# Feed-forward down blocks: the left 512 columns as seven products of 2x2 block sums

## Chip, cores and metric
One core of a Trainium2 chip. The metric is the device time of one execution in microseconds (us); lower is better. The kernel before takes 1081.49 us, median of three runs (1081.03 to 1081.93).

## The reference
Two transformer-like layers on 256 tokens of width 1024, in fp32. The first begins with a feed-forward part (`x = x + 0.5 * rmsnorm(swiglu(rmsnorm(x)))`) and ends with another; between them lie gated attention and state-space branches and a cross attention to `mem`. The second layer (long convolutions from computed filters, and a latent attention) follows. What the change touches is

```python
def _swiglu(h, w_gu, w_down):
    g, u = jnp.split(h @ w_gu, 2, axis=-1)
    return (jax.nn.silu(g) * u) @ w_down
```

with a hidden width of 2816, so 22 hidden tiles of 128, and an output of 256 x 1024.

## The kernel before
All large products keep fp32 accuracy by halves. A value is rounded to TensorE's short fp32 form (the high half), the rest (the low half) is what is left of it, and a product is three: high by high, high by low, low by high (`product`, L527 to L529).

**Weights** come as a stream of blocks of 128 x 2048 fp32 (1 MB). SyncE fetches block b into `w_raw[b % 3]` once the low half of block b - 3 is made, ScalarE makes `w_hi` (`round_block`, L1378 to L1385) once the data are there and TensorE is done with block b - 3, and VectorE makes `w_lo` (`low_block`, L2105 to L2109). TensorE waits for `w_lo_in`. So every engine's queue is written out by hand, and each runs in its own order; semaphores alone tie them.

**A feed-forward part** (`ffn_part` on each engine; n = 1 and 2) has 22 up blocks (each gives one hidden tile: 48 products of 256 columns into one of eight banks of 512 fp32 columns) and 11 down blocks, each of two hidden tiles by 1024 output columns. Its order on TensorE is up 0, 1, 2, down 0, up 3, then eight turns of a loop of up 4, down 1, up 5 (names of the first turn), then up 20, down 9, up 21, down 10. A down block is, for each of its two hidden tiles k, four groups i (two halves of the tokens by two of 512 columns) of three products of 512 columns, into banks 3 to 6, in which they are summed over all blocks. For its last group some products are cut into 256 + 256 columns (L762, by the table `LAST_DOWN`). Up blocks rotate through banks 0 to 2, by block number.

**A hidden tile** (`hidden_tile`, L2237 on VectorE; `gate` and `high` on ScalarE) goes: VectorE multiplies the first half of the bank by the row scale `rb` (L2246), ScalarE takes silu (L1439), VectorE multiplies it with the second half (L2249, it frees the bank), ScalarE rounds it (L1448, for a tile from the third on after the down block that used the buffer), VectorE takes the low half (L2256). `hidden_tile` has two lists of weight blocks: those whose low halves are made between L2249 and L2256, and those behind it. The root of the rows' squares is turned by TensorE within up 2 (first part) or up 1 (second).

**Other work in these queues.** In the first part VectorE also scales `mem` (L2293, `mem_normal`) around tile 20, and its low halves (L2300) follow the last tile. In the second it folds the long-convolution filters around tiles 0 to 3 and 20 to 21 (`fold_decay` L2202, `fold_difference` L2207, `fold_sum` L2221). Behind the last down block come the squares (ScalarE, L1516), the gains (VectorE, L2342), the root and the residual (L2356). In the first part TensorE has the memory's key blocks `kv0` to `kv3` beside this, in the second `filter_spectrum` (L1049), whose results ScalarE copies, and then the transposes of the new x (L626, `raw_turn`).

At the start TensorE runs one fp32 product of zeros (`stay_warm`, L631), zeroes bank 0 (L702) and takes the first block in plain fp32 (L710).

## Time and profile before

| | |
|---|---|
| median of three runs | 1081.49 us |
| profiled execution | 1082.24 us |
| its span | 1080.5 us |
| TensorE busy | 1071.7 us (99%), 8574 products |
| VectorE busy | 786.1 us (73%) |
| ScalarE busy | 608.4 us (56%) |
| DMA | 190.71 MB, 177 GB/s in the mean |

The profile is one execution as the hardware profiler recorded it. PE is TensorE, PEld its weight loads, DVE VectorE, ACT ScalarE. L527 is line 527 of the kernel. Matmuls are pipelined, so the distance from one start to the next, not a row's own duration, tells what one costs. Idle time in brackets is that of the engine just before a row, with what ended it.

### The profile page before, as it was taken

The numbers are of one execution on the slowest core, as the hardware profiler recorded it, in microseconds if no ns is written. First come the engines' busy times: TensorE is split into PE (matmuls) and PEld (weight loads), VectorE is DVE, ScalarE is ACT, GpSimd is POOL, SyncE is SP. The second block draws the span as 40 slices with busy tenths as digits, with TensorE's granted clock in tenths as the row PEclk, the third lists the DMA queues.
The fourth block names the chain that finished last, engine by engine and source line by source line (L and its number), as shares of the span: only waits on it lengthen the run. The fifth ranks groups of instructions, "written<-read, shape, count | busy, mean of one in ns | idle before, by whom it ended". The sixth has DMA issues, their size and how long they took to land.

```text
span 1080.5 us, 21149 instructions
## 1 busy us (share of the span) xinstructions
PE 1071.7 (99%) x8574; PEld 1015.7 (94%) x8574; DVE 786.1 (73%) x1109; ACT 608.4 (56%) x905; POOL 0.2 (0%) x4
## 2 busy tenths in 40 slices
PE   8999999999999999999999999999999999999998
PEld 7999999999989999999999998999999799999998
DVE  5665657989979777778678556765555887997784
ACT  5544444678676545878446546444444576655561
POOL 0000000000000000000000000000000000000000
PEclk9999999999999999999999999999999999999999
DMA  9766556455443454454646533465555356543341
GB/s 347 287 220 207 181 180 211 155 207 181 172 156 119 157 176 157 157 178 138 214 160 242 196 116 128 138 234 194 194 192 197 118 177 211 179 157 118 118 156 39
DMA packets 29297, 190.71 MB, mean 177 GB/s; under 512 B 3656, under 2 KB 4521, under 8 KB 7466
## 3 DMA queue, kind: packets, MB, share of 16 engines
q1 hardware_dynamic: 26480, 182.53, 48.6%
q10 hardware_dynamic: 2746, 7.16, 1.9%
q8 instruction: 54, 0.88, 0.3%
q14 instruction: 17, 0.14, 0.0%
HBM read 188.62 MB, written 1.05 MB: 176 GB/s over the span
## 4 chain that ended last, share of the span: by engine, by line
PE 93%; DVE 3%; ACT 2%; DMA 1%; issue 1%; SPq 0%; DVEq 0%; ACTq 0%
PE bank L527 16%; PE bank L529 16%; PE bank L528 16%; PE bank L539 11%; PE bank L540 11%; PE bank L541 11%; PE bank L626 3%; PE bank L762 1%; DVE sb_w_lo L2109 1%; DVE sb_ssd_conv L2420 1%; DMA sb_w_raw<-in_w 1%; PE bank L710 1%; PE bank L887 1%; ACT sb_w_hi L1385 1%; PE bank L1257 1%
## 5 line engine op out<-in xcount | busy, mean ns | idle before, releaser
L2109 DVE TENSOR_TENSOR sb_w_lo<-sb_w_raw,sb_w_hi 128x2048 fp32r<-128x2048 f32 x169 | 386.5, 2289 | 128.9 <-ACT sb_w_hi L1385 128.2
L1385 ACT ACTIVATE sb_w_hi<-sb_w_raw 128x2048 fp32r<-128x2048 f32 x169 | 322.9, 1910 | 31.5 <-PE bank L529 28.2
L527 PE MATMUL bank<-sb_hT_hi,sb_w_hi 128*128 128x256 f32 (+1 forms) x816 | 226.2, 277 | 0.0
L529 PE MATMUL bank<-sb_hT_hi,sb_w_lo 128*128 128x256 f32 (+1 forms) x816 | 226.1, 277 | 0.0
L528 PE MATMUL bank<-sb_hT_lo,sb_w_hi 128*128 128x256 f32 (+1 forms) x816 | 226.0, 277 | 0.0
L539 PE MATMUL bank<-sb_hT_hi,sb_w_hi 128*128 128x256 f32 (+2 forms) x744 | 213.4, 287 | 0.2 <-DVE sb_hT_lo L2186 0.2
L540 PE MATMUL bank<-sb_hT_lo,sb_w_hi 128*128 128x256 f32 (+2 forms) x744 | 206.7, 278 | 0.0
L541 PE MATMUL bank<-sb_hT_hi,sb_w_lo 128*128 128x256 f32 x744 | 206.4, 277 | 0.0
L527 PEld LDWEIGHTS bank<-sb_hT_hi,sb_w_hi 128*128 128x128 f32 (+1 forms) x816 | 152.9, 187 | 0.0
L529 PEld LDWEIGHTS bank<-sb_hT_hi,sb_w_lo 128*128 128x128 f32 (+1 forms) x816 | 152.7, 187 | 0.1
L528 PEld LDWEIGHTS bank<-sb_hT_lo,sb_w_hi 128*128 128x128 f32 (+1 forms) x816 | 152.7, 187 | 0.0
L539 PEld LDWEIGHTS bank<-sb_hT_hi,sb_w_hi 128*128 128x128 f32 x744 | 140.2, 188 | 3.8 <-issue 2.4
L540 PEld LDWEIGHTS bank<-sb_hT_lo,sb_w_hi 128*128 128x128 f32 x744 | 140.0, 188 | 1.4 <-issue 1.2
L541 PEld LDWEIGHTS bank<-sb_hT_hi,sb_w_lo 128*128 128x128 f32 x744 | 139.9, 188 | 0.0
L1439 ACT ACTIVATE sb_ffn_gate<-sb_ffn_gate 128x256 f32<-128x256 f32 x44 | 18.4, 418 | 133.4 <-DVE sb_ffn_gate L2246 133.4
L527 PE MATMUL bank<-sb_w_hi,sb_ffn_hi 128*128 128x512 f32 x156 | 61.0, 391 | 0.4 <-DVE sb_ffn_lo L2256 0.4
L528 PE MATMUL bank<-sb_w_lo,sb_ffn_hi 128*128 128x512 f32 x156 | 60.9, 390 | 0.0
L529 PE MATMUL bank<-sb_w_hi,sb_ffn_lo 128*128 128x512 f32 x156 | 60.9, 390 | 0.0
L1448 ACT ACTIVATE sb_ffn_hi<-sb_ffn_act 128x256 fp32r<-128x256 f32 x44 | 18.3, 416 | 47.7 <-PE bank L762 34.7
L528 PE MATMUL bank<-sb_w_lo,sb_hT_hi 128*128 128x256 f32 (+1 forms) x136 | 40.0, 294 | 0.0
L529 PE MATMUL bank<-sb_w_hi,sb_hT_lo 128*128 128x256 f32 (+1 forms) x136 | 39.9, 294 | 0.0
L527 PE MATMUL bank<-sb_w_hi,sb_hT_hi 128*128 128x256 f32 (+1 forms) x136 | 39.9, 294 | 0.0
(518 smaller groups left out, 2087.0 us busy)
## 6 DMA issues: line engine op xcount, KB each, us to landing
sb_w_raw<-in_w SPq DMA_DIRECT2D x169, 1024.0 KB, 4.9
sb_w_raw<-in_w SPq DMA_DIRECT2D x4, 512.0 KB, 7.6
sb_hT<-in_xT SPq DMA_DIRECT2D x2, 512.0 KB, 5.3
sb_x<-in_x SPq DMA_DIRECT2D x2, 512.0 KB, 11.6
sb_mem_xn<-in_mem ACTq DMA_DIRECT2D x1, 1024.0 KB, 6.0
sb_mem_T<-in_memT ACTq DMA_DIRECT2D x1, 1024.0 KB, 8.3
sb_post_g<-in_ffn_post_g ACTq DMA_DIRECT2D x2, 512.0 KB, 5.2
sb_decay<-in_c_decay ACTq DMA_DIRECT2D x1, 768.0 KB, 4.3
```

Of the source, the lines that this page charges most:

```text
L527: pe.matmul(o, a_hi, b_hi, start=first, stop=False)
L528: pe.matmul(o, a_hi, b_lo, start=False, stop=False)
L529: return pe.matmul(o, a_lo, b_hi, start=False, stop=last)
L539: pe.matmul(o[:, 0:width + more[0]], stat_hi, moving(move_hi, width + more[0]), start=k == 0, stop=False)
L540: pe.matmul(o[:, 0:width + more[1]], stat_hi, moving(move_lo, width + more[1]), start=False, stop=False)
L541: return pe.matmul(o[:, 0:width], stat_lo, moving(move_hi, width), start=False, stop=k == kt - 1)
L626: return pe.transpose(o, src, ident)
L710: mm = pe.matmul(o[:, i * SEQ:(i + 1) * SEQ], w[:, k, i * P:(i + 1) * P], hT[:, k, :], start=False, stop=k == KD - 1 and i == 1)
L1385: act.activation(w_hi[b % STAGES][:], w_raw[b % RING][:], ACT.Copy).then_inc(w_hi_in, 1)
L1439: act.activation(f["gate"][:, j % 2, :], f["gate"][:, j % 2, :], ACT.Silu).then_inc(S("ffn_gate"), 1)
L1448: act.activation(f["hi"][:, j % 2, :], f["act"][:, j % 2, :], ACT.Copy).then_inc(S("ffn_hi"), 1)
L2109: tt(w_lo[b % STAGES][:], w_raw[b % RING][:], f32(w_hi[b % STAGES][:]), ALU.subtract).then_inc(w_lo_in, 1)
```

## The change
For the down blocks of the first ten tile pairs in each part, the left 512 output columns are computed by seven products of 2x2 block sums instead of eight products of blocks: token halves by hidden tiles by two groups of 256 columns. VectorE makes three sums of the block's weights as they land (`mix_block`), of 512, 256 and 256 columns, one of them in place of a block, and four sums of the hidden tiles (`first_sum`, `other_sums`), of 128 columns each. ScalarE and VectorE make the halves of these too (768 and 4 x 128 columns). Each of the seven products is, as before, three, of 256 columns; they are summed in four banks, 3 to 6, over the ten blocks. ScalarE copies three half banks and VectorE joins them once, ahead of the last hidden tile (`join`, seven operations of 256 columns). The right 512 columns stay products of 512, in bank 7 and a bank that up blocks used; up blocks keep two banks. The last down block is as before, into its own banks, and its left half is added to the joined one behind it. Three banks are zeroed by products of zeros, at the start of the kernel (fp32) or in the second part's first mixed block. The host orders the weights of these blocks anew. Changed lines, each group with its indentation taken off:

```diff
@@ -141,11 +141,13 @@
+MIXED_PAIRS = PAIRS - 1
+MIXED_OF = {down_at(n, c): MIXED_PAIRS * (n - 1) + c for n in (1, 2) for c in range(MIXED_PAIRS)}
@@ -329,7 +331,16 @@
+        "joined": place(40, f"ffn{n}_joined", [P, TOK, 512]),
+        "parts": place(44, f"ffn{n}_parts", [P, 3, 256]),
+mix_raw = place(40 + LINE, "mix_raw", [P, 768])
+mix_hi = place(43 + LINE, "mix_hi", [P, 768], F32R)
+mix_lo = place(46 + LINE, "mix_lo", [P, 768], F32R)
+sum_raw = place(49 + LINE, "sum_raw", [P, 4, P])
+sum_hi = place(51 + LINE, "sum_hi", [P, 4, P], F32R)
+sum_lo = place(53 + LINE, "sum_lo", [P, 4, P], F32R)
+zero_r = place(55 + LINE, "zero_r", [P, P], F32R)
@@ -655,7 +666,7 @@
-o = claim(f"rb{n}", 3)
+o = claim(f"rb{n}", 6)
@@ -664,7 +675,7 @@
-o = claim("mem_rb", 7)
+o = claim("mem_rb", (FIRST["ffn1"] + 1) % 3)
@@ -720,8 +731,17 @@
+def open_mixed(n, q):
+    claim(f"mixed{n}.{q}", 3 + q, down_at(n, MIXED_PAIRS - 1))
+    last_bank = (FIRST[f"ffn{n}"] + 2) % 3
+    def up_bank(j):
+        return last_bank if n == 1 and j == 2 else (FIRST[f"ffn{n}"] + j % 2) % 3
@@ -732,63 +752,129 @@
-            feature_block(f"up{n}.{j}", b, 2, hT_hi, hT_lo, ready=ready, between=between)
+            feature_block(f"up{n}.{j}", b, 2, hT_hi, hT_lo, bank=up_bank(j), ready=ready, between=between)
-        o = claim_turns([f"up{n}.{j + 2 * i}" for i in range(PAIR_TURNS)], b % 3, b, turn)
+        o = claim_turns([f"up{n}.{j + 2 * i}" for i in range(PAIR_TURNS)], up_bank(j), b, turn)
-    def down_block(c, turn=0, parts=(512,), all_three=False):
+    def mixed_block(c, turn=0, parts=(512,), all_three=False):
+        first, last = c == 0, c == MIXED_PAIRS - 1
+        hi, lo = w_hi[b % STAGES], w_lo[b % STAGES]
+        top, low = slice(0, P), slice(P, SEQ)
+        b11, u2, b22, b21 = (slice(i * 256, (i + 1) * 256) for i in range(4))
+        u1, u3, u4 = (slice(i * 256, (i + 1) * 256) for i in range(3))
+        def tile_in(k):
+            pe.wait_ge(S("ffn_lo"), FF_TILES * (n - 1) + 2 * c + 1 + k + 2 * turn)
+        def plain_half(o, k, t):
+            h = slice(1024 + k * 512, 1536 + k * 512)
+            return product(o[:], f["hi"][:, k, t], f["lo"][:, k, t], hi[:, h], lo[:, h], first and k == 0, False)
+        def of_tile(q, half, k, t, m_hi, m_lo, m, closes):
+            return product(banks[3 + q][:, half * 256:(half + 1) * 256], f["hi"][:, k, t], f["lo"][:, k, t],
+                           m_hi[:, m], m_lo[:, m], False, last and closes)
+        def of_sum(q, half, i, m_hi, m_lo, m, closes):
+            return product(banks[3 + q][:, half * 256:(half + 1) * 256], sum_hi[:, i, :], sum_lo[:, i, :],
+                           m_hi[:, m], m_lo[:, m], first and q == 3, last and closes)
+        def open_bank(q):
+            if first and (n == 2 or q == 3):
+                open_mixed(n, q)
+            if first and n == 2 and q < 3:
+                pe.matmul(banks[3 + q][:], zero_r[:], hi[:, 0:512], start=True, stop=False)
+        if first:
+            claim(f"down{n}.1", 7)
+            if n == 2:
+                pe.wait_ge(S("zero_r"), 1)
+        tile_in(0)
+        plain_half(banks[7], 0, top)
+        open_bank(0)
+        of_tile(0, 0, 0, top, hi, lo, b11, False)
+        tile_in(1)
+        plain_half(banks[7], 1, top)
+        of_tile(0, 1, 1, top, hi, lo, b21, True)
+        open_bank(1)
+        of_tile(1, 1, 1, low, mix_hi, mix_lo, u4, False)
+        pe.wait_ge(S("ffn_sum_lo"), MIXED_PAIRS * (n - 1) + c + 1 + turn)
+        of_sum(1, 0, 3, hi, lo, b22, True)
+        open_bank(2)
+        of_sum(2, 0, 0, mix_hi, mix_lo, u1, False)
+        of_sum(2, 1, 1, hi, lo, u2, True)
+        open_bank(3)
+        of_sum(3, 0, 2, mix_hi, mix_lo, u3, True)
+        if first:
+            claim(f"down{n}.3", last_bank, down_at(n, PAIRS - 1))
+        plain_half(banks[last_bank], 0, low)
+        for m, (a, w) in enumerate(((f["hi"], hi), (f["hi"], lo), (f["lo"], hi))):
+            at = 0
+            for width in parts if all_three or m == 2 else (512,):
+                mm = pe.matmul(banks[last_bank][:, at:at + width], a[:, 1, low], w[:, 1536 + at:1536 + at + width],
+                               start=False, stop=False)
+                at += width
+        mm.then_inc(block_done, 1)
+    def last_down():
+        b = down_at(n, PAIRS - 1)
+        pe.wait_ge(w_lo_in, b + 1 - SPLIT_FROM)
+        at = {0: up_bank(0), 1: 7, 2: up_bank(1), 3: last_bank}
-            pe.wait_ge(S("ffn_lo"), FF_TILES * (n - 1) + 2 * c + 1 + k + 2 * turn)
-            for i in range(4):
+            pe.wait_ge(S("ffn_lo"), FF_TILES * (n - 1) + 2 * (PAIRS - 1) + 1 + k)
+            for i in (0, 2, 1, 3) if k else (1, 3, 0, 2):
-                first, last = c == 0 and k == 0, c == PAIRS - 1 and k == 1
...
+                if k == 0 and i % 2 == 0:
+                    claim(f"down{n}.{i}", at[i])
+                mm = product(banks[at[i]][:], f["hi"][:, k, t], f["lo"][:, k, t], hi[:, k, h], lo[:, k, h],
+                             k == 0 and i % 2 == 0, k == 1)
+                if k == 1 and i < 3:
-    o = [claim(f"down{n}.{i}", 3 + i, down_at(n, PAIRS - 1) if i == 3 else None) for i in range(4)]
-    down_block(0, 0, *LAST_DOWN[n][0])
+    mixed_block(0, 0, *LAST_DOWN[n][0])
-        down_block(1, turn, *LAST_DOWN[n][1])
+        mixed_block(1, turn, *LAST_DOWN[n][1])
+    up_block(FF_TILES - 2)
-    up_block(FF_TILES - 2)
-    down_block(PAIRS - 2, 0, *LAST_DOWN[n][2])
+    mixed_block(PAIRS - 2, 0, *LAST_DOWN[n][2])
-    down_block(PAIRS - 1)
+    last_down()
+for q in range(3):
+    open_mixed(1, q)
+    pe.matmul(banks[3 + q][:], zeros[:, 0:P], zeros[:], start=True, stop=False)
-    feature_block(f"kv{i}", FIRST["xa_k"] + i, 2, mem_hi, mem_lo, ready=None if i else mem_ready)
+    feature_block(f"kv{i}", FIRST["xa_k"] + i, 2, mem_hi, mem_lo, bank=(6, 5, 1, 0)[i],
+                  ready=None if i else mem_ready)
@@ -1149,12 +1235,11 @@
-at = (0, 1, 2, 7, (FIRST["cq"] + 1) % 3, (FIRST["cq"] + 2) % 3)
-    filter_spectrum(i, at[i])
+    filter_spectrum(i, 3 + i % 4)
-    filter_spectrum(i, at[i - 2])
+    filter_spectrum(i, (FIRST["cq"] + i - 5) % 3)
@@ -1382,7 +1467,13 @@
-act.activation(w_hi[b % STAGES][:], w_raw[b % RING][:], ACT.Copy).then_inc(w_hi_in, 1)
+if b in MIXED_OF:
+    act.wait_ge(S("ffn_mixed"), MIXED_OF[b] + 1 + turn)
+    act.activation(w_hi[b % STAGES][:], w_raw[b % RING][:], ACT.Copy)
+    act.activation(mix_hi[:], mix_raw[:], ACT.Copy).then_inc(w_hi_in, 1)
+else:
+    act.activation(w_hi[b % STAGES][:], w_raw[b % RING][:], ACT.Copy).then_inc(w_hi_in, 1)
@@ -1446,6 +1537,19 @@
+def sums_high(c, turn=0):
+    act.wait_ge(S("ffn_sum"), MIXED_PAIRS * (n - 1) + c + 1 + turn)
+    act.activation(sum_hi[:], sum_raw[:], ACT.Copy).then_inc(S("ffn_sum_hi"), 1)
+def part_copies():
+    for i, (q, half) in enumerate(((0, 0), (2, 0), (3, 0))):
+        o = full(act, f"mixed{n}.{q}")
+        ins = act.activation(f["parts"][:, i, :], o[:, 0:256], ACT.Copy)
+        ins.then_inc(S("ffn_parts"), 1)
@@ -1456,6 +1560,7 @@
+sums_high(0)
@@ -1466,6 +1571,7 @@
+sums_high(1)
@@ -1481,6 +1587,7 @@
+sums_high(2, turn)
@@ -1501,19 +1608,19 @@
+part_copies()
-for i in range(4):
-    o = full(act, f"down{n}.{i}")
-    if i % 2:
-        wait_read(act, f"down{n}.{i}")
-    if i:
-        act.wait_ge(S("post_ssq"), (0 if n == 1 else POST_SSQ[2]) + i)
-    act.activation(f["junk"][:], o[:], ACT.Square, accum_out=post_ssq[:, i // 2, i % 2:i % 2 + 1])\
+for m, i in enumerate((0, 2, 1, 3)):
+    wait_read(act, f"down{n}.{i}")
+    src = banks[fills[f"down{n}.{i}"][0]][:] if i % 2 else f["joined"][:, i // 2, :]
+    if m:
+        act.wait_ge(S("post_ssq"), (0 if n == 1 else POST_SSQ[2]) + m)
+    act.activation(f["junk"][:], src, ACT.Square, accum_out=post_ssq[:, i // 2, i % 2:i % 2 + 1])\
@@ -2106,7 +2213,22 @@
-    tt(w_lo[b % STAGES][:], w_raw[b % RING][:], f32(w_hi[b % STAGES][:]), ALU.subtract).then_inc(w_lo_in, 1)
+    ins = tt(w_lo[b % STAGES][:], w_raw[b % RING][:], f32(w_hi[b % STAGES][:]), ALU.subtract)
+    if b in MIXED_OF:
+        ins = tt(mix_lo[:], mix_raw[:], f32(mix_hi[:]), ALU.subtract)
+    ins.then_inc(w_lo_in, 1)
+def mix_block(b, turn=0):
+    w = w_raw[b % RING]
+    dve.wait_ge(w_landed[b % RING], 16 * (b // RING + 1 + turn))
+    p = MIXED_OF[b]
+    tt(mix_raw[:, 0:512], w[:, 0:512], w[:, 256:768], ALU.add).then_inc(S("ffn_mixing"), 1)
+    dve.wait_ge(S("ffn_mixing"), 2 * p + 1 + 2 * turn)
+    tt(w[:, 256:512], mix_raw[:, 0:256], w[:, 512:768], ALU.add).then_inc(S("ffn_mixing"), 1)
+    dve.wait_ge(S("ffn_mixing"), 2 * p + 2 + 2 * turn)
+    tt(mix_raw[:, 512:768], w[:, 256:512], w[:, 768:1024], ALU.add).then_inc(S("ffn_mixed"), 1)
@@ -2234,6 +2356,45 @@
+def first_sum(c, turn):
+    p = MIXED_PAIRS * (n - 1) + c
+    even = f["act"][:, 0, :]
+    if p:
+        dve.wait_ge(S("ffn_sum_hi"), p + turn)
+    tt(sum_raw[:, 2, :], even[:, 0:P], even[:, P:SEQ], ALU.subtract).then_inc(S("ffn_summing"), 1)
+def other_sums(c, turn):
+    p = MIXED_PAIRS * (n - 1) + c
+    even, odd = f["act"][:, 0, :], f["act"][:, 1, :]
+    dve.wait_ge(S("ffn_summing"), 2 * p + 1 + 2 * turn)
+    tt(sum_raw[:, 1, :], sum_raw[:, 2, :], odd[:, P:SEQ], ALU.add)
+    tt(sum_raw[:, 0, :], even[:, P:SEQ], odd[:, P:SEQ], ALU.subtract).then_inc(S("ffn_summing"), 1)
+    dve.wait_ge(S("ffn_summing"), 2 * p + 2 + 2 * turn)
+    tt(sum_raw[:, 3, :], sum_raw[:, 1, :], odd[:, 0:P], ALU.subtract).then_inc(S("ffn_sum"), 1)
+def sums_low(c, turn):
+    p = MIXED_PAIRS * (n - 1) + c
+    dve.wait_ge(S("ffn_sum_hi"), p + 1 + turn)
+    tt(sum_lo[:], sum_raw[:], f32(sum_hi[:]), ALU.subtract).then_inc(S("ffn_sum_lo"), 1)
+def join():
+    dve.wait_ge(S("ffn_parts"), 3 * n)
+    y, (p1, p5, p7) = f["joined"], (f["parts"][:, i, :] for i in range(3))
+    o = [banks[fills[f"mixed{n}.{q}"][0]] for q in range(4)]
+    read(tt(y[:, 0, 0:256], o[0][:, 256:512], p1, ALU.add), f"mixed{n}.0")
+    read(tt(p1, o[2][:, 256:512], p1, ALU.subtract), f"mixed{n}.2")
+    wait_read(dve, f"mixed{n}.2")
+    link(tt(p5, p5, p1, ALU.add))
+    tt(y[:, 0, 256:512], p5, o[1][:, 0:256], ALU.subtract)
+    read(tt(y[:, 1, 256:512], p5, p7, ALU.subtract), f"mixed{n}.3")
+    link(tt(p7, p7, p1, ALU.subtract))
+    read(tt(y[:, 1, 0:256], o[1][:, 256:512], p7, ALU.add), f"mixed{n}.1")
@@ -2247,6 +2408,14 @@
+mixed = j < 2 * MIXED_PAIRS
+if mixed:
+    wait_read(dve, f"up{n}.{j}", turn)
+    if j % 2:
+        other_sums(j // 2, turn)
+for b in behind:
+    if b in MIXED_OF:
+        mix_block(b, turn)
@@ -2255,6 +2424,8 @@
+if mixed:
+    (sums_low if j % 2 else first_sum)(j // 2, turn)
@@ -2263,7 +2434,10 @@
+    mix_block(b)
+else:
+    tt(zero_r[:], ident, ident, ALU.subtract).then_inc(S("zero_r"), 1)
@@ -2301,9 +2475,13 @@
-wait_read(dve, "mem_rb")
-mem_normal(0, 2)
-hidden_tile(FF_TILES - 2, [b], [b + 1], 0, [lambda: mem_normal(2, 5), lambda: mem_normal(5, 8)])
+def mem_first():
+    wait_read(dve, "mem_rb")
+    mem_normal(0, 4)
+hidden_tile(FF_TILES - 2, [b], [b + 1], 0, [mem_first, lambda: mem_normal(4, 8)])
+join()
@@ -2324,6 +2502,7 @@
+join()
@@ -2332,15 +2511,28 @@
-for i in (1, 0, 3, 2):
+y = f["joined"]
+def gained(i, src):
+    return stt(f["xn"][:, t, h], src, 0.5, post_g[:, h], ALU.mult, ALU.mult)
+for i in (0, 2):
-    if i % 2 == 0:
-        dve.wait_ge(S("post_ssq"), POST_SSQ[i_post] - 3 + i)
-    read(stt(f["xn"][:, t, h], o[:], 0.5, post_g[:, h], ALU.mult, ALU.mult), key)
+    if i == 0:
+        wait_read(dve, f"mixed{n}.1")
+    read(tt(y[:, i // 2, :], o[:], y[:, i // 2, :], ALU.add), key)
+for i in (1, 3):
+    key = f"down{n}.{i}"
+    read(gained(i, full(dve, key)[:]), key)
+    wait_read(dve, f"down{n}.{i - 1}")
+    scaled = gained(i - 1, y[:, (i - 1) // 2, :])
+    if i == 3:
+        link(scaled)
+dve.wait_ge(S("post_ssq"), POST_SSQ[i_post] - 2)
@@ -3111,6 +3303,9 @@
+for n in MIXED_OF:
+    top, low = stream[n, :, 0:1024].copy(), stream[n, :, 1024:2048].copy()
+    stream[n] = np.concatenate([top[:, 0:512], low[:, 256:512], low[:, 0:256], top[:, 512:], low[:, 512:]], axis=1)
```

## Rows read from the trace of the kernel before

**Rows 1.** The page: busy time by engine, and the chain that ended last.
```profile
PE 1071.7 (99%) x8574; PEld 1015.7 (94%) x8574; DVE 786.1 (73%) x1109; ACT 608.4 (56%) x905; POOL 0.2 (0%) x4
...
PE 93%; DVE 3%; ACT 2%; DMA 1%; issue 1%; SPq 0%; DVEq 0%; ACTq 0%
```

**Rows 2.** TensorE's timeline, one turn of the first loop: start us, us, instruction.
```profile
66.22 0.28 PE L539 MATMUL bank<-sb_hT_hi,sb_w_hi 128*128 128x256 f32 x1
...
76.75 0.39 PE L527 MATMUL bank<-sb_w_hi,sb_ffn_hi 128*128 128x512 f32 x1
...
81.53 0.40 PE L762 MATMUL bank<-sb_w_hi,sb_ffn_hi 128*128 128x256 f32 x2
...
82.24 0.29 PE L539 MATMUL bank<-sb_hT_hi,sb_w_hi 128*128 128x256 f32 x1
```

**Rows 3.** VectorE's timeline, the same turn; in brackets idle time before and its releaser.
```profile
71.60 0.42 DVE L2246 TENSOR_TENSOR sb_ffn_gate<-bank,sb_ffn_rb 128x256 f32<-128x256 f32 x1 [0.91 <-PE bank L529]
72.51 0.42 DVE L2249 TENSOR_TENSOR sb_ffn_act<-bank,sb_ffn_gate 128x256 f32<-128x256 f32 x1 [0.48 <-ACT sb_ffn_gate L1439]
...
75.29 2.29 DVE L2109 TENSOR_TENSOR sb_w_lo<-sb_w_raw,sb_w_hi 128x2048 fp32r<-128x2048 f32 x1 [1.39 <-ACT sb_w_hi L1385]
```

**Rows 4.** TensorE's timeline, in the two up blocks ahead of the first loop.
```profile
33.00 0.28 PE L539 MATMUL bank<-sb_hT_hi,sb_w_hi 128*128 128x256 f32 x1
...
41.12 0.28 PE L527 MATMUL bank<-sb_hT_hi,sb_w_hi 128*128 128x256 f32 x1
```

**Rows 5.** Timelines of ScalarE, VectorE and TensorE, head of the first part.
```profile
20.27 1.91 ACT L1385 ACTIVATE sb_w_hi<-sb_w_raw 128x2048 fp32r<-128x2048 f32 x1 [1.89 <-DMA sb_w_raw<-in_w]
...
24.88 0.42 ACT L1439 ACTIVATE sb_ffn_gate<-sb_ffn_gate 128x256 f32<-128x256 f32 x1 [0.75 <-DVE sb_ffn_gate L2246]
...
20.52 0.17 DVE L2177 TENSOR_SCALAR sb_post_eps<-sb_newton 128x2 f32<-128x2 f32 x1
22.22 2.29 DVE L2109 TENSOR_TENSOR sb_w_lo<-sb_w_raw,sb_w_hi 128x2048 fp32r<-128x2048 f32 x1 [1.52 <-ACT sb_w_hi L1385]
24.43 0.42 DVE L2246 TENSOR_TENSOR sb_ffn_gate<-bank,sb_ffn_rb 128x256 f32<-128x256 f32 x1
...
28.39 0.43 DVE L2256 TENSOR_TENSOR sb_ffn_lo<-sb_ffn_act,sb_ffn_hi 128x256 fp32r<-128x256 f32 x1 [0.48 <-ACT sb_ffn_hi L1448]
...
33.31 0.43 DVE L2249 TENSOR_TENSOR sb_ffn_act<-bank,sb_ffn_gate 128x256 f32<-128x256 f32 x1 [0.48 <-ACT sb_ffn_gate L1439]
...
26.81 0.47 PE L527 MATMUL bank<-sb_w_hi,sb_ffn_hi 128*128 128x512 f32 x1 [0.36 <-DVE sb_ffn_lo L2256]
...
32.54 0.39 PE L539 MATMUL bank<-sb_hT_hi,sb_w_hi 128*128 128x256 f32 x1
```

**Rows 6.** Timelines of ScalarE, VectorE and TensorE, head of the second part.
```profile
685.62 1.91 ACT L1385 ACTIVATE sb_w_hi<-sb_w_raw 128x2048 fp32r<-128x2048 f32 x1
...
686.09 1.22 DVE L2202 TENSOR_TENSOR sb_kfil<-sb_kfil,sb_decay 128x1024 f32<-128x1024 f32 x1
687.63 2.29 DVE L2109 TENSOR_TENSOR sb_w_lo<-sb_w_raw,sb_w_hi 128x2048 fp32r<-128x2048 f32 x1 [0.32 <-ACT sb_w_hi L1385]
...
690.68 0.39 PE L527 MATMUL bank<-sb_w_hi,sb_ffn_hi 128*128 128x512 f32 x1
```

**Rows 7.** Timelines of VectorE and TensorE, tails of both parts.
```profile
186.50 0.42 DVE L2246 TENSOR_TENSOR sb_ffn_gate<-bank,sb_ffn_rb 128x256 f32<-128x256 f32 x1 [0.96 <-PE bank L529]
...
848.49 0.69 DVE L2207 TENSOR_TENSOR sb_kdif<-sb_kfil 128x512 f32<-128x512 f32 x1
849.36 0.42 DVE L2246 TENSOR_TENSOR sb_ffn_gate<-bank,sb_ffn_rb 128x256 f32<-128x256 f32 x1 [0.18 <-PE bank L529]
...
860.13 1.94 PE L626 MATMUL bank<-sb_square,sb_x 128*128 128x128 f32 x16
```

**Rows 8.** TensorE's timeline: the first block's first records, and its longest idle stretch.
```profile
6.18 3.65 PE L710 MATMUL bank<-sb_hT,sb_w_raw 128*128 128x256 f32 x8 [0.94 <-DMA sb_w_raw<-in_w]
...
670.42 1.94 PE L626 MATMUL bank<-sb_square,sb_x 128*128 128x128 f32 x16 [1.84 <-ACT sb_kfil L1409]
```

10 lines of the change are left out of this document (removed).

## The prediction
> **What bounds the kernel now.** First the page's busy shares and its chain of waits [rows 1]: TensorE is busy for 99% of the span and is 93% of the chain, so time is gained by giving it less work, and lost where it is made to wait. Next its timeline in one turn of the feed-forward loop [rows 2]: from 66.22 to 76.75 there are 93 starts of products of 256 columns, a pitch of 0.1132 us; the 21 products of 512 columns take 81.53 - 76.75 = 4.78 us, 0.2276 each. Cost goes with columns, at the higher clock level. From 65.86 (the third row before 66.22) to 82.24 the turn takes 16.38 us. Then VectorE in the same turn [rows 3]: it has idle time before most of its steps, 0.91, 0.48, 1.39 us, and the low part that ends at 77.58 is wanted by TensorE at 82.24 only. In the loop there is room. Last the two heads and two tails of the feed-forward parts [rows 5 to 7], where there is little: at 26.81 TensorE already waits 0.36 us for the low half of the first hidden tile, and before the last tile VectorE is idle for only 0.96 and 0.18 us. The change puts its new work on VectorE and ScalarE in front of just these.
>
> **TensorE's work.** A down block was 24 products of 512 columns; it becomes 12 of 512 and 21 of 256, 768 columns less: 3 x 0.1132 = 0.34 us, in 20 blocks 6.8 us. Turns between widths cost something: a loop turn is 96 x 0.1132 for the up blocks and as much again per column for the down block, 10.87 + 5.43 = 16.30 by pitch and 16.38 by the rows, about 0.07 for one change of width and back. A mixed block has three such changes instead of one, +0.10 us (bounds 0 and 0.14); net 0.24 a block, 4.8 us in all. The second part also zeroes three banks by products of 512 columns, +0.7. The first part zeroes three with fp32 products before the first block's data are there; TensorE is idle for 0.94 us then [rows 8], and the first block's eight first records run at 3.65/8 = 0.43 us, the lower level, although the page shows a granted clock of 1.00. Three more there delay it at worst by some 2 us, or let it start warm. The wait for tile 0 hides most of that: I take +0.1, bounds -0.3 and +1.5.
>
> **VectorE's and ScalarE's work per pair.** Durations: VectorE 256 columns 0.42, 512 0.69, 1024 1.22, 2048 2.29 us [rows 3, 6, 7], so 128 is about 0.28 and 768 about 0.95; a following independent one starts 0.09 before the end, a dependent one 0.04 after it. ScalarE: 2048 1.91, 256 0.42 [rows 5], so 768 about 0.84 and 512 about 0.63. New on VectorE: three weight sums (0.69, 0.42, 0.42, each after the last), 0.87 for the low part of the sums, 0.8 for four hidden sums, 0.60 for their low part: some 4.3 us; on ScalarE some 1.3 us.
> In the loop this fits. The chain from one odd tile's first multiply to the next: 0.91 to the gating multiply [rows 3], 0.46 for its result, 0.5 to the last hidden sum and 0.3 for it, 0.5 for ScalarE's rounding of the sums, 1.93 for its rounding of a block (4.7), the low part 2.2 (6.9); the even tile 1.4, weight sums 1.5, a low part 2.2 (12.0); the hidden low half and difference 0.5, a low part 2.2, 0.9 for that of the weight sums: 15.6 us when nothing else holds it, against a TensorE turn of 16.14. It gives back 0.4 us a turn where it is late, and the low parts stay over 2.5 us ahead once settled. So the loop keeps 8 x 0.24 us in each part.
>
> **Head of the first part** [rows 5]. Block 3, the first mixed one, lands at 20.27; ScalarE rounded it at once. Now VectorE, busy to 20.69, makes the three sums one after another, to 22.33. ScalarE rounds from 22.35, then 768 columns more; VectorE's low part starts at 25.0 instead of 22.22 and has 0.87 more behind it, so tile 0's first multiply is at 28.1 instead of 24.43: 3.7 late. TensorE waits for that tile's low half: block starts at 30.5, not 26.81. Before tile 1's low half come the difference of tile 0 and three sums, two of them dependent, about 0.75, so it ends near 33.0; TensorE, after 1.0 us of work, stands for 1.6 more. Then the bank: the fourth plain product goes into the bank of up block 2 and waits for tile 2's multiply. That was at 33.31; it is 3.7 + 0.75 later, plus the low part of the sums (0.6) behind ScalarE's rounding of them: done near 38.7. TensorE is there at 35.8: 2.9 us. Up block 3 starts near 40.2 instead of 32.54, +7.6 net of the saving within.
>
> **Head of the second part** [rows 6]. The ScalarE rounding of the first mixed block at 685.62 waits for the sums, to 686.6, and is 0.75 longer; the low part at 687.63 becomes 689.3 and ends at 692.4, while TensorE wants it at 690.5: with the semaphore 2.0. VectorE also has filter folding behind each of the first four tiles (1.22 us at 686.09, more in later ones), so it stays behind: tile 1 1.1, block of up 4 1.6, later ones 0.6, tile 0's bank 0.1. Together 5.4 us of waits.
>
> **Tails** [rows 7]. The join is seven operations of 256 columns, 2.8 us with their links, and waits for three copies (about 1.1 us) that stand in ScalarE's queue behind the roundings and, in the first part, behind the memory's. It lies ahead of the last tile in VectorE's queue. In the first part VectorE ran 0.96 us ahead there; it now comes 2 us later out of the loop (weight sums), joins for 2.8, and gets to the last tile 3.2 us after up block 21 is done. The last down block has 2.04 us of work that doesn't need it, the same by which the old order hid the tile's latency; then it wants the last tile's bank, then its low half: 3.1 us of waits. In the second part the idle before was 0.18 and folding lies between, so 4.4 us. After the last product the residual has two adds more and squares that wait for them: about 0.9 us longer. The second part's transposes at 860.13 follow the residual closely and take 0.8 of it; the first part's are covered by the memory blocks, 0.1.
>
> **Sum.** Heads: 8.0 of waits in the first (7.6 + 0.34, the block's saving being counted below) and 5.4; tails 3.1 + 4.4 + 0.9; zero products 0.7 + 0.1; less 4.8: 17.8 us. The profiled execution is 1082.24 us with a span of 1080.5, 0.75 above the median; a difference is added to the median, 1081.49 + 17.8 = 1099.3. A measurement of this kernel can tell about 0.2% from no change, 2.2 us.
>
> **Two rules weighed.** The columns' pitch [rows 2] is proportional to width. The Trainium skill (TensorE: Matmul & The Clock Gate, Back-to-back issue gap) gives a sustained spacing of about 81 ns at 128 columns and 131 at 512 for streams with a weight load each. By interpolation, an estimate from that page, the twelve replaced products would cost 1.57 us and the twenty-one 2.05, a loss of 0.5 us a block where the sum has a gain. The trace disagrees, with 0.2276 and 0.1132, so it gets no chance.
> The stalls forecast here reach 3.7 and 4.2 us; the longest idle stretch the trace has between products is 1.84 us, and the clock doesn't fall after it [rows 8]. Whether it falls after a longer one no row shows. The Trainium skill (the same page, HAM oscillation) says that idle gaps of TensorE let the clock gate halve it again; rival 4 is what that would be here.
>
> **Rivals.**
> 1. The new work is hidden, only columns count. For it: 73% busy VectorE, idle time in the loop. Against: the head, where TensorE already waits [rows 5]. 1081.5 - 4.8 + 0.8 = 1077.5. This is the other side; it decides if heads' and tails' waits together are under 4 us instead of 21.8. Chance 0.07.
> 2. The tails stay covered: the join comes early enough (ScalarE's copies aren't held up), and the last down block hides the last tile as it did: 1099.3 - 7.5 = 1091.8. Chance 0.13, of which 0.02 stands for still fewer waits and no measurable change.
> 3. The slow pitch. The same 256 columns have a pitch of 0.1177 us from 33.00 to 41.12 [rows 4] (69 starts), with nothing else different. If the mixed block hands that on to the loops, 96 x 0.0044 x 16 = +6.8, 1106. For it: new changes of width; against: its last products are those of before, after which the loop had the fast pitch in each turn. Chance 0.10.
> 4. A fallen clock after the long stalls. By eight records at 0.43 instead of 0.21, 1.8 us an episode; two episodes 1103. Chance 0.12.
> 5. The loops are bound by VectorE's chain: at 16.4 us instead of 15.6 it never catches up and costs 0.26 in each of 16 turns: 1103.5. Chance 0.08.
> Forecast as summed: 0.50. Its own bounds (the changes of width, the zero products, half a microsecond in each of six waits) are 1096 to 1102. The range takes in rivals 2 to 5: 1091.5 to 1106. Faster 0.07, the same 0.02, slower 0.91.
>
> **What would show it.** Idle time of TensorE in the down blocks at both heads (3.6 and 1.6 for the low halves of tiles 0 and 1; 2.0 and 1.1), 2.9 on a bank after up block 2, 2.9 and 4.2 on the last tile's multiply; a loop turn of 16.1 us; up block 3 at 40.2. If TensorE has no such idle, or VectorE's queue is earlier than I put it at 28.1 for tile 0, the forecast is wrong.

## The result, and the profile after

The changed kernel takes 1103.81 us (median of 4 runs, 1102.93 to 1104.4) beside 1081.26 of the kernel before: a ratio of 1.0207, with a 95% interval of 1.0194 to 1.0219. That is 22.5 us slower, where 17.8 were forecast. The profiled execution took 1104.12 us with a span of 1102.3, 21.8 over the span before. One execution of the experiments below, of the three orders together, was disturbed (4108.61 us) and is left out of its kernel's median.

The page of the changed kernel, its busy row, TensorE's granted clock in 40 slices, and the chain that ended last:

```profile
PE 1076.7 (98%) x8763; PEld 1025.9 (93%) x8763; DVE 869.6 (79%) x1308; ACT 638.5 (58%) x951; POOL 0.2 (0%) x4
...
PEclk9899999999999999999999999999999899999999
...
PE 82%; DVE 9%; ACT 4%; issue 3%; DMA 1%; SPq 0%; ACTq 0%; DVEq 0%
```

Against [rows 1], VectorE has 83.5 us more work in 199 more instructions and rose from 3% to 9% of the chain. The two slices of the clock that show an 8 are the head of the first part and the tail of the second. TensorE's busy time *rose* by 5 us although it has fewer columns: part of it is work at the lower clock.

**A loop turn**, TensorE's timeline of the changed kernel: up block, mixed block, next turn.

```profile
745.53 0.29 PE L550 MATMUL bank<-sb_hT_hi,sb_w_hi 128*128 128x256 f32 x1
...
756.43 0.39 PE L538 MATMUL bank<-sb_w_hi,sb_ffn_hi 128*128 128x512 f32 x1
...
757.12 0.28 PE L538 MATMUL bank<-sb_w_hi,sb_ffn_hi 128*128 128x256 f32 x1
757.24 0.28 PE L539 MATMUL bank<-sb_w_lo,sb_ffn_hi 128*128 128x256 f32 x1
...
761.73 0.29 PE L550 MATMUL bank<-sb_hT_hi,sb_w_hi 128*128 128x256 f32 x1
```

The turn is 761.73 - 745.53 = 16.20 us against 16.38 [rows 2]. The forecast was 16.14. The mixed block takes 5.30 us; the old one took 5.49 (82.24 - 76.75). It saves 0.19, where 0.24 was forecast.

**Head of the first part**, timelines of ScalarE, VectorE and TensorE:

```profile
22.18 1.92 ACT L1473 ACTIVATE sb_w_hi<-sb_w_raw 128x2048 fp32r<-128x2048 f32 x1 [3.94 <-DVE sb_mix_raw L2231]
...
20.46 0.69 DVE L2227 TENSOR_TENSOR sb_mix_raw<-sb_w_raw 128x512 f32<-128x512 f32 x1
...
24.86 2.29 DVE L2216 TENSOR_TENSOR sb_w_lo<-sb_w_raw,sb_w_hi 128x2048 fp32r<-128x2048 f32 x1 [2.80 <-ACT sb_mix_hi L1474]
...
27.94 0.42 DVE L2407 TENSOR_TENSOR sb_ffn_gate<-bank,sb_ffn_rb 128x256 f32<-128x256 f32 x1
...
38.14 0.43 DVE L2410 TENSOR_TENSOR sb_ffn_act<-bank,sb_ffn_gate 128x256 f32<-128x256 f32 x1 [0.48 <-ACT sb_ffn_gate L1530]
...
30.39 0.76 PE L538 MATMUL bank<-sb_w_hi,sb_ffn_hi 128*128 128x512 f32 x1 [4.02 <-DVE sb_ffn_lo L2425]
30.95 0.63 PE L539 MATMUL bank<-sb_w_lo,sb_ffn_hi 128*128 128x512 f32 x1
...
38.62 0.50 PE L538 MATMUL bank<-sb_w_hi,sb_ffn_hi 128*128 128x512 f32 x1 [1.19 <-DVE sb_ffn_act L2410]
...
40.12 0.29 PE L550 MATMUL bank<-sb_hT_hi,sb_w_hi 128*128 128x256 f32 x1
```

Beside [rows 5]: ScalarE's rounding waits for the weight sums, VectorE's low part starts at 24.86 instead of 22.22, tile 0's multiply at 27.94 instead of 24.43 (28.1 was forecast), and the down block at 30.39 instead of 26.81 (30.5). The fourth triple of products of 512 columns stands until tile 2's multiply frees the bank of up block 2, and up block 3 starts at 40.12 (40.2). New is the pitch behind the first wait: the second and third products of 512 columns start at 30.95 and, in the next row of the trace, at 31.38, 0.43 us apart instead of 0.23. That is the clock's lower level (granted clock 0.54 in the window below). The slow products fill time in which TensorE would have stood: it waits 0.28 us for tile 1, where 1.6 were forecast, and 1.2 for the bank, where 2.9 were.

**Head of the second part**, VectorE and TensorE:

```profile
700.39 2.29 DVE L2216 TENSOR_TENSOR sb_w_lo<-sb_w_raw,sb_w_hi 128x2048 fp32r<-128x2048 f32 x1 [1.19 <-ACT sb_mix_hi L1474]
702.60 0.95 DVE L2218 TENSOR_TENSOR sb_mix_lo<-sb_mix_raw,sb_mix_hi 128x768 fp32r<-128x768 f32 x1
...
703.61 0.50 PE L538 MATMUL bank<-sb_w_hi,sb_ffn_hi 128*128 128x512 f32 x1 [1.70 <-DVE sb_mix_lo L2218]
...
706.05 0.50 PE L538 MATMUL bank<-sb_w_hi,sb_ffn_hi 128*128 128x512 f32 x1 [0.88 <-DVE sb_ffn_lo L2425]
...
717.67 0.38 PE L550 MATMUL bank<-sb_hT_hi,sb_w_hi 128*128 128x256 f32 x1 [1.19 <-DVE sb_w_lo L2216]
```

The first mixed block waits 1.7 us for the low part of the weight sums, then 0.9 for tile 1, and up block 4 waits 1.2 for its low part (forecast 2.0, 1.1, 1.6), against [rows 6].

**The tails**: VectorE, from the join on, and TensorE; the last row is the second part's transposes.

```profile
193.02 0.42 DVE L2389 TENSOR_TENSOR sb_ffn_joined<-bank,sb_ffn_parts 128x256 f32<-128x256 f32 x1
...
195.73 0.41 DVE L2407 TENSOR_TENSOR sb_ffn_gate<-bank,sb_ffn_rb 128x256 f32<-128x256 f32 x1
...
197.11 0.50 PE L538 MATMUL bank<-sb_w_hi,sb_ffn_hi 128*128 128x512 f32 x1 [2.49 <-DVE sb_ffn_act L2410]
...
213.32 0.38 PE L550 MATMUL bank<-sb_mem_hi,sb_w_hi 128*128 128x256 f32 x1 [0.93 <-DVE sb_w_lo L2216]
...
868.88 0.41 DVE L2407 TENSOR_TENSOR sb_ffn_gate<-bank,sb_ffn_rb 128x256 f32<-128x256 f32 x1
...
870.25 0.80 PE L538 MATMUL bank<-sb_w_hi,sb_ffn_hi 128*128 128x512 f32 x1 [3.58 <-DVE sb_ffn_act L2410]
870.84 0.63 PE L539 MATMUL bank<-sb_w_lo,sb_ffn_hi 128*128 128x512 f32 x1
...
882.39 1.94 PE L637 MATMUL bank<-sb_square,sb_x 128*128 128x128 f32 x16 [0.73 <-ACT sb_half L1500]
```

In [rows 7] the last tile's first multiply was at 186.50 and 849.36, hardly behind the up block. Now it comes 3.3 and 4.4 us behind the last up block (192.40, 864.45), behind the join. TensorE does the nine products that it can, stands for 2.5 and 3.6 us, and in the second part goes on at 0.43 us a product of 512 columns for twelve products. The same by windows, the first head and the second tail (busy time per engine, then TensorE's granted clock, DMA share, GB/s):

```profile
31.00:36.50 5.50, 5.22 (x21) 4.44 (x20) 3.70 (x7) 3.08 (x4) 0.00 (x0) 0.54 0.73 259
...
870.30:876.40 6.10, 6.10 (x16) 4.85 (x17) 3.57 (x6) 3.65 (x6) 0.00 (x0) 0.55 0.01 1
```

### The profile page after: what moved, and what is told of

Same layout as the page of the kernel before. It is cut to its first block, busy times and chain, and to the rows that moved or that the text cites. A ratio compares the mean times of both kernels' runs of the same rounds, so it can differ in the third digit from the quotient of the medians.

```text
span 1102.3 us, 21890 instructions
## 1 busy us (share of the span) xinstructions
PE 1076.7 (98%) x8763; PEld 1025.9 (93%) x8763; DVE 869.6 (79%) x1308; ACT 638.5 (58%) x951; POOL 0.2 (0%) x4
## 4 chain that ended last, share of the span: by engine, by line
PE 82%; DVE 9%; ACT 4%; issue 3%; DMA 1%; SPq 0%; ACTq 0%; DVEq 0%
PE bank L538 14%; PE bank L539 14%; PE bank L540 14%; PE bank L550 10%; PE bank L551 9%; PE bank L552 9%; DVE sb_w_lo L2216 3%; PE bank L637 3%; ACT sb_w_hi L1476 1%; PE bank L827 1%; DVE sb_ssd_conv L2612 1%; DMA sb_w_raw<-in_w 1%; ACT sb_w_hi L1473 1%; PE bank L973 1%; PE bank L1342 1%
## 5 line engine op out<-in xcount | busy, mean ns | idle before, releaser
L538 PE MATMUL bank<-sb_w_hi,sb_ffn_hi 128*128 128x512 f32 (+1 forms) x116 | 44.0, 379 | 14.2 <-DVE sb_ffn_act L2410 7.3
L539 PE MATMUL bank<-sb_w_lo,sb_ffn_hi 128*128 128x512 f32 (+1 forms) x116 | 43.0, 371 | 0.0
L540 PE MATMUL bank<-sb_w_hi,sb_ffn_lo 128*128 128x512 f32 (+1 forms) x116 | 42.7, 368 | 0.0
L1473 ACT ACTIVATE sb_w_hi<-sb_w_raw 128x2048 fp32r<-128x2048 f32 x20 | 38.4, 1918 | 7.1 <-DVE sb_mix_raw L2231 6.5
L538 PEld LDWEIGHTS bank<-sb_w_hi,sb_ffn_hi 128*128 128x128 f32 x116 | 23.1, 199 | 19.1 <-DVE sb_ffn_act L2410 8.3
L2612 DVE SCALAR_TENSOR_TENSOR sb_ssd_conv<-bank,sb_cols,sb_ssd_conv 128x255 f32<-128x255 f32 (+2 forms) x72 | 34.7, 482 | 6.7 <-ACT sb_ssd_conv L1719 4.5
```

The lines of the kernel that those rows point to most:

```text
L538: pe.matmul(o, a_hi, b_hi, start=first, stop=False)
L539: pe.matmul(o, a_hi, b_lo, start=False, stop=False)
L540: return pe.matmul(o, a_lo, b_hi, start=False, stop=last)
L1473: act.activation(w_hi[b % STAGES][:], w_raw[b % RING][:], ACT.Copy)
L2612: ins = stt(v[:, j:SEQ], u[:, 0:SEQ - j], col("ssd_conv_w", taps * ch + taps - 1 - j), v[:, j:SEQ], ALU.mult, ALU.add)
```

## The experiments

What was open: whether the join's place makes the tails' waits, what the fallen clock cost at either end, why a mixed block saves less than reckoned, and how the 22.5 us divide among VectorE's new work, the join and the banks. Each difference below is a kernel's median minus that of the kernel before in the same comparison (1081.5, 1082.0 or 1081.5). The changed kernel's own is +22.5.

### Join behind the last tile

```diff
-                    join()
                     hidden_tile(FF_TILES - 1, [], [])
+                    join()
```
(second part; in the first it stands ahead of `mem_low(0)`, behind tile 21, and `kv0` takes bank 3.)

> The changed kernel with the join behind the last hidden tile in VectorE's queue instead of ahead of it, in both parts, and the first memory block in bank 3, which the join's first operation frees. Theory (the join stands in front of the last tile and is what TensorE waits for in the last down block, 3.1 us in the first part, 3.7 in the second, and the fallen clock behind the second wait costs 2.6 more): the last down block takes 5.5 to 6 us in both parts, all its products of 512 columns stay at 0.23 us, and what is left is a shorter wait of the first memory block and of the residual for the join: 6 to 9 us less than the changed kernel's 1103.8, so 1095 to 1098. Rival (VectorE is so late by then that the tile waits whatever stands ahead of it, or the join only moves its 2.8 us to the residual and the memory blocks): 3 us less or nothing, 1101 to 1104.

1102.42 us, +20.9: 1.6 less than the change, where the theory wanted 6 to 9. Yet TensorE's timeline shows the theory at work in the last down blocks, and then the bill:

```profile
199.28 0.36 PE L550 MATMUL bank<-sb_mem_hi,sb_w_hi 128*128 128x256 f32 x1 [0.92 <-DVE sb_mem_lo L2474]
...
213.29 0.38 PE L550 MATMUL bank<-sb_mem_hi,sb_w_hi 128*128 128x256 f32 x1 [2.88 <-DVE sb_w_lo L2216]
...
869.13 0.50 PE L538 MATMUL bank<-sb_w_hi,sb_ffn_hi 128*128 128x512 f32 x1 [0.88 <-DVE sb_ffn_act L2410]
...
881.15 1.94 PE L637 MATMUL bank<-sb_square,sb_x 128*128 128x128 f32 x16 [1.00 <-DVE sb_x L2548]
```

The first part's last down block ended at 198.2 instead of 200.93. But `kv0` then waited for the memory's low halves behind the join, and `kv2` stood for 2.9 us for its weight block, whose low half is made behind the residual in VectorE's queue. Behind that wait the clock fell (products of 256 columns 0.21 us apart from 214.1 to 217.3; the window 213.30 to 217.40 has a granted clock of 0.59), so that the first part ended 1.6 us *later* than in the changed kernel. In the second part the wait shrank from 3.6 to 0.9 us and the clock stayed up: from the last down block's start the filter's first product came after 7.9 us instead of 11.9, the transposes after 15.1 instead of 17.9, since the residual had to wait for the join. So the theory holds for where the wait is. It fails on what it is worth: in the first part VectorE is the bound from there to `kv2`.

### TensorE kept at work in the tail

```diff
+                        if n == 2 and k == 0:
+                            for _ in range(16):
+                                pe.matmul(banks[7][:], zero_r[:], hi[:, 1, 0:512], start=False, stop=False)
```

> The changed kernel with 16 products of 512 columns of a zero tile, added to an open bank at the start of the second part's last down block (3.7 us at 0.228 each), so that TensorE works through what was its wait for the last tile. The result is the same. Theory (the clock fell because TensorE stood still for 3.7 us; the twelve products behind the wait then take 0.43 us each instead of 0.23): these products run at 0.23 us, the last down block ends at the changed kernel's time less 2.4 to 2.6 us, the kernel takes 1101.2 to 1101.5. Rival (the slow products have another cause, such as the first use of the bank, the operands of the last tile or VectorE's traffic at that time): they stay at 0.43 and the time stays at 1103.8, or grows by up to 0.5.

1102.43 us, +20.9. TensorE's timeline:

```profile
864.47 3.80 PE L842 MATMUL bank<-sb_w_hi,sb_zero_r 128*128 128x512 f32 x16
...
870.27 0.50 PE L538 MATMUL bank<-sb_w_hi,sb_ffn_hi 128*128 128x512 f32 x1
```

The same kernel's windows, columns as above, the first of them at the first part's tail:

```profile
198.10:201.60 3.50, 3.49 (x9) 2.76 (x9) 3.50 (x4) 1.35 (x1) 0.00 (x0) 0.51 0.00 0
...
864.40:870.20 5.80, 5.80 (x28) 4.57 (x26) 5.21 (x11) 0.42 (x1) 0.00 (x0) 1.00 0.82 305
870.20:874.10 3.90, 3.90 (x17) 2.85 (x17) 3.35 (x6) 3.21 (x5) 0.00 (x0) 1.00 0.01 2
```

The group behind the wait starts at 870.27, as before (870.25), and ends at 874.09 instead of 876.34, at a granted clock of 1.00. The fallen clock cost 2.25 us there, and the profiled span is 2.3 us shorter; the medians differ by 1.4 to 1.6. The rival falls: same bank, same operands, same VectorE, and the products are fast. The first of the windows shows that in this execution the clock fell at the first part's tail too, behind the same wait of 2.49 us that left it up in the changed kernel, although the two kernels differ only in the second part. Nothing of that was left at the second part's first up block (683.98 against 683.96 us), so it does not touch the comparison above.

### Rounding that doesn't wait for the sums

```diff
-                    act.wait_ge(S("ffn_mixed"), MIXED_OF[b] + 1 + turn)
-                    act.activation(w_hi[b % STAGES][:], w_raw[b % RING][:], ACT.Copy)
+                    for c in (slice(0, 256), slice(512, 2048)):
+                        act.activation(w_hi[b % STAGES][:, c], w_raw[b % RING][:, c], ACT.Copy)
+                    act.wait_ge(S("ffn_mixed"), MIXED_OF[b] + 1 + turn)
+                    act.activation(w_hi[b % STAGES][:, 256:512], w_raw[b % RING][:, 256:512], ACT.Copy)
```

> The changed kernel with ScalarE's rounding of a mixed block cut in three: the 1792 columns that the weight sums don't rewrite at once on landing, then the other 256 and the 768 sums behind the weight sums. Theory (at the heads ScalarE stands still behind VectorE's weight sums, 2.1 us in the first part and 1 in the second, and this is part of what TensorE waits for): the low part of the first mixed block starts 1.2 to 1.5 us earlier at the first head, the first down block 1.2 to 1.5 earlier than 30.39, up block 3 earlier than 40.12 by as much; at the second head 0.5 to 1.2 less; the kernel 1101 to 1102. If the first wait becomes short enough for the clock to stay at its upper level, nothing more is gained there, since the bank of up block 2 comes last. Rival (VectorE's own queue is what counts, ScalarE's start is not): within 0.5 us of 1103.8.

1101.33 us, +19.8, within the theory's range. At the second head the down block starts at 701.88 - 683.38 (up block 0) = 18.50 us instead of 703.61 - 683.96 = 19.65, with 0.5 us of wait instead of 1.7. At the first the gain was 0.45 only: in that execution block 3 landed at 21.55, at least 1.1 us later than in the changed kernel's profile (20.46 or before), which can have hidden the rest. The clock fell all the same.

### One change of width less

```diff
                     open_bank(0)
-                    of_tile(0, 0, 0, top, hi, lo, b11, False)
+                    if first:
+                        of_tile(0, 0, 0, top, hi, lo, b11, False)
                     tile_in(1)
                     plain_half(banks[7], 1, top)
+                    if not first:
+                        of_tile(0, 0, 0, top, hi, lo, b11, False)
```

> The changed kernel with the first product of each mixed block but the first of a part (256 columns) moved behind the second product of the right half (512 columns), so that the block has one change of width to and fro less. Theory of the prediction (a change of width and back costs 0.07 us): a loop turn of 16.13 instead of 16.20 us, 18 x 0.07 = 1.2 us less, 1102.6. Rival (the triples of 256 columns of a mixed block run at 0.119 us a product wherever they stand, since each of them has other stationary and moving tiles than the one before; the change of width costs nothing): the turn stays at 16.20 and the kernel at 1103.8.

1103.31 us, +21.8, and a turn of 172.16 - 155.96 = 16.20. The rival is right in this: a change of width costs nothing that the turn shows.

### All products of 256 columns into one place

```diff
+                        o = banks[3 + q][:, half * 256:(half + 1) * 256] if first or last else banks[3][:, 0:256]
```

> The changed kernel, where all seven products of 256 columns of each mixed block but the first and the last of a part go into the same half of one bank, so that the join's input is no longer the seven products. TensorE's work, waits and everything else stay. Theory (a triple of 256 columns costs 0.358 us instead of the 0.340 of the up blocks because each triple goes to another bank or half than the one before): the triples fall to 0.340, the loop turn from 16.20 to 16.07 us. Rival (the cost lies in the kind of product, hidden tile held still and weights moving, or in the change of the moving tile at each product): the turn stays at 16.20.

One execution, 1104.49 us. Part of a mixed block, and the turn:

```profile
152.85 0.28 PE L538 MATMUL bank<-sb_mix_hi,sb_ffn_hi 128*128 128x256 f32 x1
...
153.20 0.28 PE L538 MATMUL bank<-sb_w_hi,sb_sum_hi 128*128 128x256 f32 x1
...
156.05 0.29 PE L550 MATMUL bank<-sb_hT_hi,sb_w_hi 128*128 128x256 f32 x1
...
172.25 0.29 PE L550 MATMUL bank<-sb_hT_hi,sb_w_hi 128*128 128x256 f32 x1
```

The turn is 16.20 and a triple takes 0.35 to 0.36 us: the bank isn't it either. The next suspicion is the kind of product: in the mixed block the hidden tile is held and the weights move (0.119 us for 256 columns), in the up block it is the other way about (0.1132). The kernel before clears it, since it has long runs of the first kind as well:

```profile
559.27 0.28 PE L539 MATMUL bank<-sb_w_hi,sb_mixed_hi 128*128 128x256 f32 x1
...
580.92 0.28 PE L529 MATMUL bank<-sb_w_hi,sb_mixed_lo 128*128 128x256 f32 x1
```

These 191 starts are (580.92 - 559.27) / 191 = 0.1133 us apart. With `sb_late` held the pitch is 0.1134 from 581.03 to 591.80 and 0.1178 from 593.90 to 604.86. The moving tile changes at each product there and in the up blocks too, so that is not it either. Products of 256 columns run at 0.1133 or 0.1178 whichever operand is held, and the mixed block's lie near the slower of the two. What sets the pitch stays open.

### No sums at all

```diff
-                    mixed = j < 2 * MIXED_PAIRS
+                    mixed = False
```
(with `mix_block`, `sums_high`, the rounding of `mix_raw` and its low part left out, and `f["hi"]`, `f["lo"]`, `hi`, `lo` in the products in their place.)

> The changed kernel without the weight sums, the hidden sums, their roundings and their low parts: the products that read them read the block's own columns and the hidden tiles instead, of the same shapes and in the same order. It leaves out that part of the computation; the join, the banks and TensorE's work stay. Theory (the cost of the heads is VectorE's and ScalarE's new work per pair, plus in the first part a wait of its own for the bank of up block 2, whose multiply was at 33.31 already in the kernel before): tile 0's low half comes as before, the first down block starts near 26.8, its fourth product of the right half still waits until about 33.9, up block 3 starts near 35.2; the second head costs only the zero products, 0.7; the loop turn stays at 16.20; the tails lose to the join alone, 1.5 and 2.7, and 0.9 and 0.8 in the residual and the third memory block. Together 1081.3 + 2.7 + 0.7 + 5.9 - 3.8 = 1086.8, between 1084 and 1089. Rival (the waits come from the order of the products and the banks, not from the sums): over 1095, with the waits at the heads in their places.

1089.98 us, +8.0, where the theory's 1086.8 was +5.5 and its range ended at 1089. Both heads, TensorE:

```profile
27.81 0.47 PE L538 MATMUL bank<-sb_w_hi,sb_ffn_hi 128*128 128x512 f32 x1 [1.19 <-DVE sb_ffn_lo L2416]
...
29.87 0.76 PE L538 MATMUL bank<-sb_w_hi,sb_ffn_hi 128*128 128x512 f32 x1 [0.78 <-DVE sb_ffn_lo L2416]
...
34.78 0.50 PE L538 MATMUL bank<-sb_w_hi,sb_ffn_hi 128*128 128x512 f32 x1 [0.27 <-DVE sb_ffn_act L2402]
...
36.27 0.29 PE L550 MATMUL bank<-sb_hT_hi,sb_w_hi 128*128 128x256 f32 x1
...
701.62 0.29 PE L550 MATMUL bank<-sb_hT_hi,sb_w_hi 128*128 128x256 f32 x1
```

Block 3 landed about 1 us late here too (its low part started at 23.22, not at 22.22), so up block 3 is at 36.27, where 35.2 was reckoned. It is 3.7 us behind the kernel before with none of VectorE's new work; about 1 of these is the late landing. The clock fell here too, behind a wait of 0.78 us that followed one of 1.19. The second head costs 701.62 - 678.00 = 23.62 against 696.17 - 673.35 = 22.82 before, 0.8, about the zero products. The last down blocks still wait 1.5 and 1.9 us. The rival (banks and order, over 1095) is refuted as a whole, but most of what is left at the first head is its: 35.2, with block 3 on time, is 2.7 behind the kernel before, and it was reckoned from the bank alone.

### Tile 2 ahead of up block 3's low half

```diff
-                    hidden_tile(1, [], [b + 1])
-                    hidden_tile(2, [b + 2], [b + 3])
+                    hidden_tile(1, [], [])
+                    hidden_tile(2, [b + 1, b + 2], [b + 3])
```

> The changed kernel with the low part of up block 3 moved behind tile 2's two multiplies in VectorE's queue, in the first part only. Theory (up block 3 starts at 40.12 because the fourth product of the right half waits for the bank of up block 2, which tile 2's multiply frees at 38.6 behind that low part of 2.29 us): the multiply ends near 36.3, TensorE, which gets there at 37.3, waits no more, and up block 3 waits for its own low part, done near 38.8, and starts at 38.8 to 39: 1.1 to 1.3 us less, 1102.6. Rival 1 (ScalarE's roundings or the landing of the blocks hold the low part back, and it comes later still): no gain, or a loss of up to 1. Rival 2 (the low clock at the first down block is the cost, not the bank): up block 3 stays at 40.1.

1102.99 us, +21.0. The bank is free in time: TensorE runs from 38.41 to 38.53 without a wait. But up block 3 starts at 40.11, as in the changed kernel, because this execution's down block began 0.44 later (30.83) and the slow clock lasted until 38.4, since no wait for the bank hid it any more. Within the execution the path from the down block to up block 3 is 9.28 us instead of 9.73. So rival 2 is right in part: with the bank out of the way, the low clock is what counts next. The medians give 0.8 to 1.5 us, of which this place shows 0.45; the rest is not traced.

### TensorE kept at work in the first head

```diff
+                    if first and n == 1:
+                        pe.wait_ge(S("zero_r"), 1)
+                        for _ in range(16):
+                            pe.matmul(banks[3][:], zero_r[:], hT_hi[:, 0:2, :], start=False, stop=False)
                     pe.wait_ge(w_lo_in, b + 1 - SPLIT_FROM + TURN * turn)
```

> The changed kernel with 16 products of 512 columns of a zero tile ahead of the first part's first down block, added to an open bank, so that TensorE works through its wait of 4 us for the block and for tile 0. The result is the same. Theory (the clock falls there as it does in the second part's tail, but the products that it slows end before the bank of up block 2 comes free, so that it costs nothing): the products from 30.4 on run at 0.23 and 0.12 us instead of 0.43 and 0.21, they are done some 1.8 us earlier, the wait for the bank is longer by as much, up block 3 starts at 40.1 to 40.4 (the zero tile takes 0.28 us of VectorE) and the kernel takes 1103.8 to 1104.1. Rival (the low clock is part of what the head costs): up block 3 starts 1 to 2 us earlier, 1102 to 1103.

1104.66 us, +22.7. The windows, with the granted clock third from the end:

```profile
26.00:36.50 10.50, 8.08 (x45) 6.57 (x43) 7.43 (x14) 4.11 (x6) 0.00 (x0) 1.00 0.51 163
36.50:39.30 2.80, 0.21 (x3) 0.02 (x1) 2.28 (x4) 0.95 (x2) 0.00 (x0) 0.95 1.05 433
39.30:42.60 3.30, 3.30 (x11) 2.82 (x12) 3.23 (x4) 1.62 (x3) 0.00 (x0) 0.52 0.98 395
```

TensorE's timeline of it:

```profile
39.28 0.80 PE L538 MATMUL bank<-sb_w_hi,sb_ffn_hi 128*128 128x512 f32 x1 [2.59 <-DVE sb_ffn_act L2414]
...
42.01 0.41 PE L550 MATMUL bank<-sb_hT_hi,sb_w_hi 128*128 128x256 f32 x1
```

The products of the down block run fast now, and nothing is gained: TensorE reaches the bank sooner, waits 2.6 us for it, and the clock falls there, where no later wait hides it. Up block 3 starts at 42.0 instead of 40.1. Of these 1.9 us 0.66 have another source: the first mixed block landed later in this execution, and tile 2's multiply freed the bank at 39.28 instead of 38.62. The changed kernel's fallen clock at this head was free, as the theory said; what it hadn't foreseen is that filling one wait moves the fall to the next.

### Three orders together

The changes of the first (second part only), third and seventh experiments in one kernel.

> The changed kernel with three orders changed and no work left out: the join behind the last hidden tile in the second part only, a mixed block's rounding cut in three so that most of it doesn't wait for the weight sums, and the low part of up block 3 behind tile 2's multiplies in the first part. Theory (each works where it was measured or expected alone: 2.3 to 2.9 at the second tail, since the clock stays up, 1.8 at the second head and 0.4 to 1.4 at the first, 1.2 at the bank of up block 2): 1096 to 1098. Rival (they overlap: at the first head all three waits stand behind the same queue of VectorE, and the join's 2.8 us come back in the residual): 1099 to 1101. Neither expects it to reach the kernel before.

1098.38 us (median of three), +16.4, a ratio of 1.0153 (1.0133 to 1.0173): 6.2 less than the change, between the theory's 1096 to 1098 and the rival's 1099 to 1101. Here the first part's tail has a wait of 2.6 us and the clock falls behind it, from 197.04 to 200.0, where the changed kernel with a wait of 2.5 kept it. The order of things is worth a quarter of the loss, no more.

### What the parts weigh

```diff
-                    act.wait_ge(S("ffn_mixed"), MIXED_OF[b] + 1 + turn)
-                    act.activation(mix_hi[:], mix_raw[:], ACT.Copy).then_inc(w_hi_in, 1)
-                    ins = tt(mix_lo[:], mix_raw[:], f32(mix_hi[:]), ALU.subtract)
```
(without weight sums)

> The changed kernel without the weight sums, their rounding and their low part; the hidden sums stay, the products that read the weight sums read the block's own columns. It leaves out that part of the computation. Without all sums the kernel took 1090.0. Theory (by their times in the queues: the weight sums are 1.6 + 0.9 us of VectorE and 0.8 of ScalarE a pair, the hidden sums 0.8 + 0.6 and 0.6, and at both heads the former stand ahead of the first product that TensorE waits for): up block 3 starts at 37.5 to 37.8, the second head costs 2 us or less, the stall of the second tail is short enough for the clock to stay up, 1093 to 1096. Rival (the hidden sums matter more, since they lie between a tile's multiply and its low half in every pair): up block 3 stays at 39 or later, 1099 or more.

```diff
-                    read(tt(y[:, 0, 0:256], o[0][:, 256:512], p1, ALU.add), f"mixed{n}.0")
+                    read(tt(f["parts"][:, 0, 16:32], o[0][:, 256:272], p1, ALU.add), f"mixed{n}.0")
```
(without the join, the other six operations alike; and two copies by ScalarE)

> The changed kernel with the join's seven operations cut to 16 columns each, and the joined sums filled by two copies of ScalarE instead, so that the join as a computation is left out. All else stays. Theory (VectorE's 2.8 us ahead of the last hidden tile are most of both waits in the last down blocks): the first wait falls from 2.65 to about 0.4 us, the second from 3.75 to about 1.5, the clock stays up behind it (2.6), the kernel takes 1103.8 - 2.3 - 2.3 - 2.6 = 1096.6. Rival (the tile is late through the weight sums in VectorE's queue, the join only fills time): over 1101.

> The changed kernel without any sums of weights and hidden tiles and without the join, each replaced as in the two kernels that leave out one of them: what is left of the change are TensorE's products, the zero products, the banks and the two further additions in the residual. Theory (the parts add): 1090.0 less the 1.7 and 2.1 us that its last down blocks still waited, 1086; of the 4 us over the kernel before, 3.7 are the first head's bank and low clock and the rest the zero products (0.7), the residual and the third memory block (1.7) and two late hidden tiles, less 20 x 0.19 = 3.8. Rival (TensorE's products themselves cost something that the loop turn doesn't show): 1088 or more. A time below 1081.5 would say that the change pays once the sums are free.

| kernel | median, us | over the kernel before |
|---|---|---|
| changed kernel | 1103.81 | 22.5 |
| without the join | 1101.44 | 20.0 |
| without weight sums | 1093.32 | 11.9 |
| without weight and hidden sums | 1089.98 | 8.0 |
| without sums and join | 1085.54 | 4.1 (ratio 1.0038, 1.0025 to 1.0051) |

The weight sums weigh 10.6 us, the hidden sums another 3.9, the join 3.9 on top of these. The shares hold for this order of leaving out: with the join left out first it weighs 2.5 and the sums 15.9. Without weight sums up block 3 starts at 37.62, as expected (by luck in part, since the first mixed block landed 1 us late, at 21.27), and the second head costs 703.55 - 679.43 = 24.12, 1.3 over before. That is the theory, within its range (1093 to 1096), though not in its detail: the second tail still waited 3.0 us and the clock did fall. Without the join alone the gain was 2.5 instead of 7.2, and the time is in the rival's range (over 1101). TensorE in that kernel:

```profile
196.76 0.50 PE L538 MATMUL bank<-sb_w_hi,sb_ffn_hi 128*128 128x512 f32 x1 [1.55 <-DVE sb_ffn_act L2412]
...
868.43 0.64 PE L538 MATMUL bank<-sb_w_hi,sb_ffn_hi 128*128 128x512 f32 x1 [1.84 <-DVE sb_ffn_act L2412]
868.86 0.63 PE L539 MATMUL bank<-sb_w_lo,sb_ffn_hi 128*128 128x512 f32 x1
```

The waits are 1.6 and 1.8 us instead of 2.5 and 3.6, since seven narrow, linked operations still take 1.0 us and the first waited 0.7 for ScalarE's copies; and the clock fell behind the wait of 1.8 all the same, and in this execution also at the second head (from 706.1 on). So cutting the join to 1.0 us took 0.9 us off the first wait and 1.7 off the second, where the theory had 2.3 for each, and the theory's clock term is not there. Without sums and join, where 1086 was expected, the tails wait 0.75 and 0.17, and 4.1 us are left with VectorE's sums and join gone. Up block 3 starts at 36.94, 4.4 behind the kernel before: 0.6 were there when the down block began (27.45), the rest is late hidden tiles, TensorE's wait of 1.8 us for the bank of up block 2, and the clock that fell behind it.

## Why the prediction was right, and where it was not

Set against the spans of the two profiles (21.8):

| term | forecast | measured |
|---|---|---|
| first head, up block 3 | 7.6 (+0.34) | 7.58 (+0.2) |
| zero products, first part | 0.1 | -0.2 (up block 1 at 14.48), part of the row above |
| first tail | 3.1 | 3.1 |
| second head, with its zero products | 6.1 | 6.6 |
| second tail | 4.4 | 3.8, and 2.6 for the clock |
| residual, memory blocks | 0.9 | 0.6 and 0.8 |
| 20 blocks | -4.8 | -3.8 |

The first tail's is the last down block from 192.40 to 200.93, 8.53 us against 5.45. The second's is 870.25 - 866.5 = 3.75 of standing still (the next product would have come at 866.5), and 876.34 - 870.25 = 6.09 for fifteen products that take 3.45 at the upper level. The second head is the growth of the lead from 10.61 us at up block 0 to 16.59 at 745.53, with three savings of 0.19 added back. The measured rows add up to 21.5. A scan step adds 0.6 and the first part's loop 0.2 (both below); 0.4 come back behind the transposes.

**Right**: the bound, the side, and the mechanism step by step. VectorE's queue at the first head was forecast to 0.2 us over 20 us (at the second the first mixed block's low part came 0.5 later than forecast), and the walk of waits (block, tile 0, tile 1, bank of up block 2) is that of the trace. Their sizes are not: tile 1 cost 0.28 us of standing instead of 1.6 and the bank 1.2 instead of 2.9, since the products between ran at the lower clock. The end of the block was right all the same, because VectorE's multiply sets it and not TensorE. The loop absorbed the new work but for 0.4 us in the first turn, so rival 5 is out. Rivals 1 and 2 are out by the waits seen.

**The saving was a fifth too large.** The step on the turns between widths took the 0.08 us by which the old turn exceeded its pitches for a price of the change of width. The fourth experiment removed one such change and got nothing. The cost is in the products: 21 at 0.1194 instead of 0.1132 are 0.13 us a block, and the twelve of 512 columns, at 0.2325 instead of 0.2276, bring it to about the 0.15 that 0.34 - 0.19 leaves, where the sum had 0.10; 1.0 us in all. The sum took the fastest pitch of each width. The trace of before has slower ones with an activation held: 0.1178 for 256 columns (593.90 to 604.86) and 0.2333 for 512 (48 products from 1055.08 to 1066.28). With these the mixed block would take 21 x 0.1178 + 12 x 0.2333 = 5.27 us, and it took 5.30. So it runs close to rival 3's slow pitch, which the prediction weighed only as something that the block might hand on to the loop.

**The fallen clock was a rival with 0.12, and it happened.** Its two episodes are there, at the places where the forecast's own waits were longest, at 3.6 and 4.0 us. One was covered (experiment on the first head), the other cost 2.3 to 2.6. The forecast put its waits of 3.7 and 4.2 us beside a longest idle of 1.84 in [rows 8] and then priced the sum as if nothing lay between. The step that failed is the split into "as summed" and "rival 4": the likeliest case should have had the second tail's episode in it, 1.8 to 2.6, and would have read 1101 to 1102. The forecast's own bounds, 1096 to 1102, missed; the range held the time because rivals 3 to 5 were in it. That the measured 1103.8 lies near rival 4's 1103 is in part luck: the rival pays two episodes of 1.8, the run paid one of 2.3 to 2.6, and the saving (1.0), the second head (0.5) and the small terms below made up the rest. By the rule cited there (the Trainium skill, TensorE: Matmul & The Clock Gate, HAM oscillation), the trace agrees: granted clock 0.55 behind 3.6 us, and 1.00 when the same 3.6 us were filled. Behind shorter waits the runs went either way (last section).

**Smaller.** The forecast of 0.1 for the first part, its transposes covered by the memory blocks, was wrong: it is not the transposes but `kv2`'s low half that follows the residual in VectorE's queue. In the kernel before it ended at 203.25, with `kv2` at 203.32, without slack; the two adds move it by 0.8. Another 0.6 comes at a scan step (at 302 us in the kernel before), where TensorE waits for VectorE, 1.5 us against 0.5 there, and in the step behind it. Rival 3's slow pitch (0.1178) did appear, in up blocks 2, 4, 5 and 6 of the second part, 190 products or 0.8 us (part of the second head's 6.6), and in up block 6 of the first, 0.2 us, while up blocks 3 and 4 of the first part, slow in [rows 4], became fast (0.4 us back). Together with the first turn's 0.4 that leaves the 0.2 of the first part's loop. What sets which pitch a block gets stays open; it changed from one kernel to the next in the same place. The division 3.65/8 in the prediction gives 0.46, not 0.43; the first seven starts are 0.43 us apart but for the first distance, so the level it read is right.

The experiments also divide the loss, which the prediction did not: left out in this order, 14.5 of 22.5 us are the sums, 3.9 the join, and 4.1 stay even when both are gone. So in this order of banks the change did not pay even then. Up block 3 was 4.4 us late at the first head, more than the 3.8 that twenty blocks save. How much of that is the up blocks' third bank is not shown, since no kernel gives it back; the estimate of 35.2 for up block 3 makes it 2.7.

## What to carry to other kernels

A trade of TensorE's columns for VectorE's work is decided where VectorE has no lead: at the first and last blocks of a stage, and not in its loop, however idle that looks. Price a saved product not by the pitch of the one loop it stands in, but by the slowest and the fastest that products of its width show anywhere in the trace. A forecast wait longer than any that the trace has should carry a fallen clock behind it in the likeliest case, unless a later wait covers it; and when such a wait is filled or shortened, look where TensorE stands next.

## What the hardware showed that was not expected

- The clock's fall did not go by the length of the wait just before it. It fell behind waits of 4.0, 3.6, 3.0 (without weight sums), 2.9, 2.6 (three orders), 1.8 (without the join) and 0.78 us (no sums, 1.19 shortly before it), and not behind 1.9 (no sums, second tail) or 1.8 (without weight sums, first tail). The same wait in the same place went both ways: 2.49 us at the first tail left the clock up in the changed kernel and brought it down in the second experiment's, which is the same up to there (granted clock 0.51 in its first window). So one profile doesn't tell whether a wait of 1.8 to 2.6 us costs the clock. The second head's two waits of 1.7 and 0.9 us left it up in the changed kernel; in the kernel without the join it fell there. In some the products ran at the upper level at first: with three orders six of them did at the first tail, without weight sums four at the second.
- At the upper level of the clock products of 256 columns have two pitches in long runs, 0.1133 and 0.1178 us, whichever operand is held, and those of 512 columns 0.2276 and 0.2333. Mixed blocks lay near the slower ones (0.1194 and 0.2325).
- The landing of the first mixed block varied by 2.6 us between the profiles of the different kernels, from 19.78 (three orders) to 22.38 (one place), and with it the first head: up block 3 started at 42.06 in the latter.
